# A mixture-of-experts layer in fp32: two experts' token columns gathered at once, and the down products by column halves

## The chip, the cores and the metric

The kernel runs on one core of one Trainium2 chip. The metric is the device time of one execution in microseconds (us). One core is used, so there is no exchange with others.

## The reference

One layer of a decoder on 256 tokens of width 1024: a mixer (a gated convolution beside chunked gated linear attention), then a mixture of 32 experts of which each token uses 4, then a final RMS norm. The part that matters here is the experts:

```
logits = xf @ w_router + b_router            # 256 x 32
top_v, top_i = lax.top_k(logits, 4);  gates = softmax(top_v)
for each expert e, for the tokens that chose it:
    gu   = x_e @ w_gate_up[e] + b_gate_up[e]         # 1024 -> 2048
    gate = min(gu[:, :1024], 7);  up = clip(gu[:, 1024:], -7, 7)
    glu  = gate * sigmoid(gate * 1.702)
    y[tokens] += gate_weight * (((up + 1) * glu) @ w_down[e] + b_down[e])
out = rmsnorm(x + y)
```

All numbers are float32. An expert has 1024 x 2048 weights for gate and up and 1024 x 1024 for down, 12.58 MB together, and the 32 experts have 402.7 MB. Everything is read once.

## The kernel before, in words

The mixer and the router run first, about 123 us. Then one pass over the experts, each as an item of at most 64 tokens (SLOTS; what more tokens an expert has goes to extra items after the last expert, of which this input needs none). An expert's weights are 6 chunks of 2.1 MB: chunks 0 to 3 hold gate and up, 4 and 5 hold down. A ring of 12 slots holds two experts' chunks. SyncE (SP) issues the loads in order on one queue; each waits until TensorE has counted the chunk that lay in its slot as used (`s_used`). Experts 6 to 13 and 22 to 27 are loaded in pairs of chunks (4 MB, line 572; at both edges of these ranges some more pairs, line 599), experts 14 to 21 in fours (8 MB, line 560); the first experts and the last two are loaded in chunks and smaller pieces. TensorE waits on the semaphore of a slot before the first product of its chunk.

What TensorE does for expert `it` is written out by hand in `products` and is the same for all experts:

- `gate_up`: 4 chunks, each 4 blocks of 128 rows, for each of which the 64 token columns `x_t` are the stationary operand and 512 weight columns the moving one, twice (two halves of the array side by side). Between the chunks it turns the gate matrix of this expert (`turn_gates`, result `p_t`) and, when ScalarE has copied a bank, the products (`turn`).
- `down`: 2 chunks, products into bank 0, 512 columns wide; VectorE and ScalarE make the activations meanwhile.
- `gather_next`: the rows of the next expert's tokens are picked out of `xs` by a 0/1 matrix `p_row` that VectorE made (scaled by the norm's factor), into bank 3. ScalarE copies them to `x_row`, TensorE turns them (`turn_gathered`, 4 transposes), and VectorE multiplies them by the norm's weights into `x_t`.
- `scatter`: ScalarE has copied bank 0 to `z`; the products of `p_t` and `z` are added to four banks y that hold the output of all 256 tokens.

The code for experts 0 and 1 is written out, that for 2 to 29 is a hardware loop over pairs (`InLoop`), and experts 30 and 31 are interleaved by hand in `products_last_two`, whose down weights come in pieces so that little is left after the last load. Three things are done once on the way: the down biases (`start_sums`) and the residual rows (`add_rows`) are added to the y banks in experts 4 and 5, and the final norm's weights are spread over the partitions (`broadcast_g`) in experts 12 and 13. In the program every fp32 product is two MATMUL instructions; a transpose is one.

## Time and profile before

| | before |
|---|---|
| median of 3 runs | 1015.89 us (1015.86 to 1016.98) |
| profiled execution, its own time | 1016.16 us |
| its span, first to last instruction | 1014.4 us |
| TensorE (PE) busy | 996.1 us, 98% |
| VectorE (DVE), ScalarE (ACT) busy | 284.5 us, 152.8 us |
| memory moved | 423.86 MB, mean 418 GB/s |
| chain that ended last, by engine | PE 87%, DMA 11% |

Busy times are sums over the instructions of an engine. The profiled execution lies 0.27 us over the median. TensorE works through a queue in order, and the end of a matmul is modelled, so that two engines (TensorE and the 16 DMA engines) can both look full; which of them the other waits for has to be read from single waits.

### The profile page before, as it was taken

To read this page: it belongs to the slowest core of one execution; us is meant where nothing else is said; L and a number is where in the kernel's file an instruction comes from. 1 tells how busy PE (TensorE), PEld (TensorE's weight loads), DVE (VectorE), ACT (ScalarE), POOL (GpSimd) and SP (SyncE) were. 2 spreads that over 40 slices of the span, in tenths; PEclk is the share of its full clock that TensorE was granted. 3 is DMA by queue.
4 is the path that set the end of the run, shared out by engine and by line. 5 is a ranking of instruction groups with operands and counts; after the bars stand their busy time and mean duration, and the time that the engine had idled before them with its cause. 6 is when DMAs were issued, how large, how long until landed. Compare 5 with 4: busy or idle time off the path is not lost.

```text
span 1014.4 us, 12715 instructions
## 1 busy us (share of the span) xinstructions
PE 996.1 (98%) x4940; PEld 414.9 (41%) x4940; DVE 284.5 (28%) x692; ACT 152.8 (15%) x324; POOL 14.8 (1%) x31
## 2 busy tenths in 40 slices
PE   9999999999999999999999999999999999999997
PEld 8889734333333333333333333332333333333334
DVE  4997522222221222222221122211222222122122
ACT  2421311111111111111111111111111111111112
POOL 3010000000000000000000000000000000000000
PEclk9999999999999999999999999999999999999999
DMA  9986999999999999999999999999999999999997
GB/s 368 426 371 263 390 402 425 427 433 425 430 432 432 433 425 434 430 433 442 437 432 432 437 429 439 429 439 421 424 434 430 433 433 432 433 421 431 426 419 283
DMA packets 23510, 423.86 MB, mean 418 GB/s; under 512 B 2872, under 2 KB 3520, under 8 KB 8000
## 3 DMA queue, kind: packets, MB, share of 16 engines
q1 hardware_dynamic: 22464, 422.09, 97.7%
q10 hardware_dynamic: 1024, 1.47, 0.4%
q8 instruction: 14, 0.23, 0.1%
q14 instruction: 8, 0.07, 0.0%
HBM read 422.51 MB, written 1.05 MB: 418 GB/s over the span
## 4 chain that ended last, share of the span: by engine, by line
PE 87%; DMA 11%; SPq 1%; issue 1%; DVE 0%; ACT 0%; POOLq 0%; POOL 0%; ACTq 0%; DVEq 0%; PEldq 0%
PE bank L2000 38%; PE bank L2027 20%; PE y L2071 5%; PE bank L1860 5%; DMA ring<-in_w_expert 5%; DMA ring<-in_w_fours 4%; PE bank L1628 4%; PE bank L2045 3%; DMA ring<-in_w_down_last 3%; PE y L1803 2%; PE bank L1935 2%; PE bank L1704 1%; PE bank L1621 1%; PE bank L2051 1%; PE y L1614 1%; PE bank L1803 1%
## 5 line engine op out<-in xcount | busy, mean ns | idle before, releaser
L2000 PE MATMUL bank<-ring,x_t 128*64 128x512 f32 x1984 | 447.3, 597 | 0.3 <-DVE x_t L1442 0.3
L2000 PEld LDWEIGHTS bank<-ring,x_t 128*64 128x64 f32 x1984 | 134.1, 137 | 262.6 <-issue 260.4
L2027 PE MATMUL bank<-ring,act 128*64 128x512 f32 (+1 forms) x968 | 224.6, 596 | 4.4 <-DMA ring<-in_w_fours 2.3
L1482 DVE TENSOR_TENSOR gu_b<-bank,bias_t 128x512 f32<-128x512 f32 x64 | 44.3, 692 | 322.4 <-PE bank L2045 322.4
L2027 PEld LDWEIGHTS bank<-ring,act 128*64 128x64 f32 x968 | 67.5, 137 | 129.8 <-issue 129.6
L931 ACT COPY gu_sb<-bank 128x512 f32<-128x512 f32 x64 | 37.4, 585 | 222.9 <-PE bank L2000 222.9
L1435 DVE TENSOR_TENSOR x_t<-bank,cols 128x512 f32<-128x512 f32 x30 | 20.7, 691 | 165.1 <-PE bank L1935 165.1
L2071 PE MATMUL y<-z,p_t 64*128 64x512 f32 (+1 forms) x248 | 59.7, 601 | 0.0
L1860 PE MATMUL bank<-x_sb,p_row 128*64 128x512 f32 x248 | 58.5, 592 | 0.0
L1421 DVE TENSOR_SCALAR p_row<-slot,rank,rstd 128x64 f32<-128x64 f32 x62 | 16.6, 311 | 147.7 <-PE bank L2051 147.7
L935 ACT ACTIVATE act<-gu_b 128x256 f32<-128x256 f32 x62 | 25.8, 416 | 190.4 <-DVE gu_b L1488 190.4
L2045 PEld LDWEIGHTS bank<-ident,gu_sb 128*128 128x128 f32 x256 | 26.8, 140 | 51.7 <-issue 51.3
L2045 PE MATMUL bank<-ident,gu_sb 128*128 128x128 f32 x256 | 42.0, 286 | 0.1
L927 ACT COPY p_t<-bank 128x256 f32<-128x256 f32 x31 | 11.5, 373 | 185.7 <-PE bank L2051 185.7
L1860 PEld LDWEIGHTS bank<-x_sb,p_row 128*64 128x64 f32 x248 | 17.8, 137 | 35.4 <-issue 35.4
L939 ACT COPY z<-bank 128x512 f32<-128x512 f32 x30 | 17.6, 586 | 85.5 <-PE bank L2027 85.5
L2071 PEld LDWEIGHTS y<-z,p_t 64*128 64x128 f32 x248 | 21.6, 186 | 18.8 <-issue 13.7
L1498 DVE TENSOR_TENSOR act<-act,gu_b 128x256 f32<-128x256 f32 x62 | 26.4, 425 | 6.5
L1493 DVE SCALAR_TENSOR_TENSOR gu_b<-gu_b 128x256 f32<-128x256 f32 x64 | 27.2, 425 | 2.2
L923 ACT COPY x_row<-bank 128x512 f32<-128x512 f32 x31 | 18.1, 585 | 63.0 <-PE bank L1860 63.0
L1935 PEld LDWEIGHTS bank<-ident,x_row 128*128 128x128 f32 x124 | 13.0, 141 | 31.2 <-issue 31.2
L1935 PE MATMUL bank<-ident,x_row 128*128 128x128 f32 x124 | 19.5, 280 | 4.8 <-PE bank L2027 4.6
(311 smaller groups left out, 549.1 us busy)
## 6 DMA issues: line engine op xcount, KB each, us to landing
ring<-in_w_expert SPq DMA_DIRECT2D x48, 4096.0 KB, 24.4
ring<-in_w_expert SPq DMA_DIRECT2D x33, 2048.0 KB, 14.6
ring<-in_w_expert SPq DMA_DIRECT2D x16, 1024.0 KB, 9.3
ring<-in_w_in SPq DMA_DIRECT2D x4, 2048.0 KB, 25.3
ring<-in_w_down_last SPq DMA_DIRECT2D x10, 512.0 KB, 19.6
ring<-in_w_out SPq DMA_DIRECT2D x2, 2048.0 KB, 27.4
ring<-in_w_expert SPq DMA_DIRECT2D x8, 512.0 KB, 6.4
ring<-in_w_down_last SPq DMA_DIRECT2D x3, 1024.0 KB, 35.7
```

Source lines behind the costliest of these rows:

```text
L931: act_e.copy(gu_sb[:, h, :], bank[h][:, :]).then_inc(s_guk, 1)
L1482: dve.tensor_tensor(gu_b[:, :, :, :], bank[2][:, :].rearrange("p (f a s) -> p a f s", a=2, f=4), bias_t[:, :, 4 * h:4 * h + 4, ds(e, 1)] . ...
L1493: dve.scalar_tensor_tensor(out=gu_b[:, 1, :, :], in0=gu_b[:, 1, :, :], scalar=1.0, in1=gu_b[:, 0, :, :], op0=ALU.add, op1=ALU.mult).then_i ...
L1498: dve.tensor_tensor(act_of(it)[:, 4 * h:4 * h + 4, :], act_of(it)[:, 4 * h:4 * h + 4, :], gu_b[:, 1, :, :], ALU.mult).then_inc(s_av, 1)
L1628: ins = mm(acc.rearrange("p a n -> p (a n)"), h[:, k, :], w[:, k, :], start=first and k == 0, stop=last and k == 3, skip_group_check=True)
L1803: ins = mm(acc, y[:, k, :], w[:, k, :], start=first and k == 0, stop=last and k == CT - 1, skip_group_check=True)
L1860: ins = mm(bank[3][a * SLOTS:(a + 1) * SLOTS, :], p_row[:, t, :], xs[:, t, a * HALF:(a + 1) * HALF], start=t == 0, stop=t == TT - 1)
L1935: ins = nc.tensor.transpose(bank[3][:, f * P:(f + 1) * P], x_row[:, f * P:(f + 1) * P], ident[:, :])
L2000: ins = mm(bank[h][a * SLOTS:(a + 1) * SLOTS, :], x_t_of(it)[:, k, :], w[:, kk, a, :], start=k == 0, stop=k == KT - 1)
L2027: ins = mm(bank[0][a * SLOTS:(a + 1) * SLOTS, c], act_of(it)[:, k, :], w[:, kk, a, c], start=k == 0, stop=k == KT - 1)
L2045: ins = nc.tensor.transpose(bank[2][:, f * P:(f + 1) * P], gu_sb[:, h, f * P:(f + 1) * P], ident[:, :])
L2071: ins = mm(y_ps[t][nn][:, c], p_t_of(it)[r, t * P:(t + 1) * P], z[r, c], start=first, stop=False, skip_group_check=True)
```

## The change

Four things.

- For experts 2 to 31 the token columns of two experts are gathered at once (`gather_pair`, in experts 1, 3, 5, ... 29): now `xs` is the stationary operand (128 x 128) and the two experts' 0/1 matrices side by side, `p_rows`, are the moving one (128 columns), so that the columns come out turned. The copy to `x_row`, the 4 transposes and the wait between them are gone. VectorE makes `x_pair` out of bank 3 in two halves (`keep_pair`), the second product waits for the first half.
- The down products are made by column halves: all rows of the chunk for columns 0 to 255 into bank 0, then for columns 256 to 511 into bank 1; ScalarE copies `z` in two halves, and `scatter` adds it in two halves.
- The spread of the final norm's weights (`broadcast_g`) moves from experts 12 and 13 to expert 30, the down biases (`start_sums`) from expert 4 to expert 1.
- In the first scatter only the first half resets a y bank. `bdn` lies elsewhere and is loaded after the gate biases and once the gates are there, not before them.

The core of the diff:

```diff
@@ build
-        gu_sb, x_t, p_row, p_gate = row((("gu_sb", [P, 2, HALF], f32), ("x_t", [P, KT, SLOTS], f32),
-                                         ("p_row", [P, TT, SLOTS], f32), ("p_gate", [P, TT, P], f32)), 8192, 16384)
+        gu_sb, x_pair = row((("gu_sb", [P, 2, HALF], f32), ("x_pair", [P, KT, 2, SLOTS], f32)), 8192, 16384)
+        x_t = at("x_t", [P, KT, SLOTS], 12288)
+        bdn = at("bdn", [P, HALF], 14336)
@@ load_biases (SP)
-                sp.wait_ge(s_lg, 2)
-                sp.dma_start(bdn[:, :], b_down).then_inc(s_bdn, 16)
                 sp.wait_ge(s_p0, 3)
                 sp.dma_start(bias_t[:, :, :, :], b_gate_up.rearrange("p (a f e) -> p a f e", a=2, f=F // P)).then_inc(s_bias, 16)
+                sp.wait_ge(s_gtk, 1)
+                sp.dma_start(bdn[:, :], b_down).then_inc(s_bdn, 16)
@@ ScalarE
-            def keep_z(it):
-                act_e.wait_ge(s_dn, it + 1)
-                act_e.copy(z[:, :], bank[0][:, :]).then_inc(s_z, 1)
+            def keep_z(it, extra):
+                for h in range(2):
+                    c = slice(h * QUARTER, (h + 1) * QUARTER)
+                    act_e.wait_ge(s_dn, down_done(it, h, extra))
+                    act_e.copy(z[:, c], bank[h][:, 0:QUARTER]).then_inc(s_z, 1)
@@ VectorE
+            def keep_pair(it):
+                for h in range(2):
+                    dve.wait_ge(s_xg, it + (2 + h))
+                    dve.tensor_tensor(x_pair[:, 4 * h:4 * h + 4, :, :].rearrange("p k o s -> p k (o s)"),
+                                      bank[3][:, :].rearrange("p (k s) -> p k s", k=4),
...
+                                      .broadcast_to([P, 4, P]), ALU.mult).then_inc(s_xt, 1)
@@ TensorE, down
-                    for a in range(2):
-                        for c in column_parts(it) if k in (5, 6) else (slice(0, HALF),):
-                            ins = mm(bank[0][a * SLOTS:(a + 1) * SLOTS, c], act_of(it)[:, k, :], w[:, kk, a, c],
-                                     start=k == 0, stop=k == KT - 1)
+                    for a in range(2):
+                        ins = mm(bank[h][a * SLOTS:(a + 1) * SLOTS, 0:QUARTER], act_of(it)[:, k, :], w[:, kk, a, c],
+                                 start=k == 0, stop=k == KT - 1)
@@ TensorE
+            def gather_pair(it, h):
+                if h == 0:
+                    pe.wait_ge(s_p, number(it) + 2)
+                    pe.wait_ge(s_ptk, number(it) + 1)
+                else:
+                    pe.wait_ge(s_xt, number(it) + 2)
+                for k in range(4 * h, 4 * h + 4):
+                    for t in range(TT):
+                        ins = mm(bank[3][:, k % 4 * P:(k % 4 + 1) * P], xs[:, t, k * P:(k + 1) * P],
+                                 p_rows[:, t, :, :].rearrange("p o s -> p (o s)"), start=t == 0, stop=t == TT - 1)
+                ins.then_inc(s_xg, 1)
@@ products
+                if known == 1:
+                    start_sums()
+                if isinstance(it, InLoop) and it.odd == 0:
+                    pe.wait_ge(s_xt, number(it) + 2)
...
-                down(it, 4, range(0, 2))
+                down(it, 4, 0, range(0, 2), extra)
                 turn(it, 1)
-                down(it, 4, range(2, 4))
-                if following is not None:
+                down(it, 4, 0, range(2, 4), extra)
+                down(it, 4, 1, range(4), extra)
+                next_pair = known == 1 or isinstance(it, InLoop) and it.odd == 1
+                if known == 0:
                     gather_next(it)
+                if next_pair:
+                    gather_pair(it, 0)
                 pe.wait_ge(s_av, number(it) * 2 + 2)
-                down(it, 5, range(4))
-                if following is not None:
-                    turn_gathered(following)
-                scatter(it)
+                for h in range(2):
+                    down(it, 5, h, range(4), extra)
+                if known == 0:
+                    turn_gathered(1)
+                if next_pair:
+                    gather_pair(it, 1)
+                scatter(it, extra)
```

How TensorE's instructions stand in the hardware loop, in the second expert of a pair, from the second half of chunk 2 on (a row here is a product of two instructions, or one transpose, by the source line; ring_51 is where the down chunks lie). Before:

```order
L2000 MATMUL bank<-ring_51,x_t 64x512 x12
L2027 MATMUL bank<-ring_51,act 64x512 x4
L2040 REGISTER_ALU
L2045 MATMUL bank<-ident,gu_sb 128x128 x4
L2027 MATMUL bank<-ring_51,act 64x512 x4
L2056 REGISTER_ALU
L1860 MATMUL bank<-x_sb,p_row 64x512 x4
L2027 MATMUL bank<-ring_51,act 64x512 x8
L1935 MATMUL bank<-ident,x_row 128x128 x4
L2071 MATMUL y<-z,p_t 128x512 x4
```

After:

```order
L2028 MATMUL bank<-ring_51,x_pair 64x512 x12
L2047 MATMUL bank<-ring_51,act 64x256 x4
L2062 REGISTER_ALU
L2067 MATMUL bank<-ident,gu_sb 128x128 x4
L2047 MATMUL bank<-ring_51,act 64x256 x12
L2102 REGISTER_ALU
L2108 MATMUL bank<-p_rows,x_sb 128x128 x8
L2047 MATMUL bank<-ring_51,act 64x256 x16
L2108 MATMUL bank<-p_rows,x_sb 128x128 x8
L2094 MATMUL y<-z,p_t 128x256 x8
```

The gather of 4 wide products and the 4 transposes became 16 products of 128 columns in two groups; in the first expert of a pair both are gone. Down has 32 products of 256 columns where it had 16 of 512, the scatter 8 where it had 4.

TensorE's instructions in expert 1, from its start to its first turned products, before:

```order
L2000 MATMUL bank<-ring_50,x_t 64x512 x8
L2051 MATMUL bank<-ident,p_gate 128x128 x2
L2000 MATMUL bank<-ring_50,x_t 64x512 x8
L2000 MATMUL bank<-ring_51,x_t 64x512 x4
L2045 MATMUL bank<-ident,gu_sb 128x128 x4
```

And after:

```order
L2028 MATMUL bank<-ring_50,x_t 64x512 x8
L2005 MATMUL y<-bdn,gates_t 128x512 x4
L2073 MATMUL bank<-ident,p_gate 128x128 x2
L2028 MATMUL bank<-ring_50,x_t 64x512 x8
L2028 MATMUL bank<-ring_51,x_t 64x512 x4
```

The 4 products of the down biases now stand after the expert's first chunk; they stood in expert 4.

SyncE's queue around the two bias loads, with what each waits for (first_p_row_ready is `s_p0`, gates_t_ready is `s_gtk`). Before:

```order
L579 DMA early_quarter<-in_w_expert 128x1024 [waits partial_logits_ready]
L552 DMA ring_51<-in_w_expert 128x1024 [waits block_product_ready]
L583 DMA bdn<-in_b_down 128x512 [waits logits_ready]
L585 DMA bias_t<-in_b_gate_up 128x512 [waits first_p_row_ready]
L552 DMA ring_49<-in_w_expert 128x1024 [waits first_chunks_quarter_used] x3
```

After:

```order
L593 DMA early_quarter<-in_w_expert 128x1024 [waits partial_logits_ready]
L566 DMA ring_51<-in_w_expert 128x1024 [waits block_product_ready]
L597 DMA bias_t<-in_b_gate_up 128x512 [waits first_p_row_ready]
L599 DMA bdn<-in_b_down 128x512 [waits gates_t_ready]
L566 DMA ring_49<-in_w_expert 128x1024 [waits first_chunks_quarter_used] x3
```

The load of `bdn` moved behind that of `bias_t` and has another wait; the first refill of a ring slot stands right behind it. From there on SyncE's queue is the same, load by load.

## Rows read from the trace of the kernel before

**Rows 1.** The page: the engines' busy time, and TensorE's group that waits most.

```profile
PE 996.1 (98%) x4940; PEld 414.9 (41%) x4940; DVE 284.5 (28%) x692; ACT 152.8 (15%) x324; POOL 14.8 (1%) x31
...
L2027 PE MATMUL bank<-ring,act 128*64 128x512 f32 (+1 forms) x968 | 224.6, 596 | 4.4 <-DMA ring<-in_w_fours 2.3
```

**Rows 2.** Waits of SyncE's queue: total us, times, longest.

```profile
SPq L572 <- PE bank L2000: 233.9, 28, 9.9
```

**Rows 3.** DMA view of 150 to 210 us: rate, and loads with median us to landing.

```profile
DMA packets 2069, 25.58 MB, mean 426 GB/s; under 512 B 234, under 2 KB 234, under 8 KB 234
...
ring<-in_w_expert SPq DMA_DIRECT2D x11, 2048.0 KB, 12.4
```

**Rows 4.** The same view of 730 to 850 us.

```profile
DMA packets 1780, 51.81 MB, mean 432 GB/s; under 512 B 199, under 2 KB 199, under 8 KB 199
...
ring<-in_w_expert SPq DMA_DIRECT2D x14, 4096.0 KB, 42.8
```

**Rows 5.** Chain from 290 to 350 us: start us, us, what.

```profile
292.39 3.58 PE bank L2000 x16
...
311.70 1.72 PE bank L1860 x8
313.42 3.46 PE bank L2027 x16
...
317.01 0.63 PE bank L1935 x4
317.64 1.92 PE y L2071 x8
319.55 3.59 PE bank L2000 x16
```

**Rows 6.** Chain in the mixer, 128 x 128 products of 128 columns (two instructions each).

```profile
76.29 5.36 PE bank L1621 x48
```

**Rows 7.** Chain in expert 1, whose down and scatter are partly in halves.

```profile
171.57 3.51 PE bank L2027 x24
...
175.85 2.03 PE y L2071 x16
```

**Rows 8.** Chain: down biases in expert 4, one half of the final weights' spread.

```profile
240.01 1.07 PE y L1977 x8
...
462.93 1.08 PE bank L2115 x8
```

**Rows 9.** Windows: stretch, its us, busy times, clock share, DMA share, GB/s last.

```profile
122.00:126.00 4.00, 3.71 (x22) 1.49 (x21) 1.73 (x7) 1.59 (x2) 0.00 (x0) 1.00 0.78 243
134.00:138.00 4.00, 4.00 (x22) 1.37 (x20) 1.37 (x5) 0.42 (x1) 0.00 (x0) 1.00 1.04 432
```

**Rows 10.** Timeline around 122 us: the gates, and the first refills.

```profile
122.08 0.22 DVE L1414 TENSOR_TENSOR gates<-ex,ngt 128x64 f32<-128x64 f32 x1
...
124.21 24.09 SPq L552 DMA_DIRECT2D ring<-in_w_expert  x15
```

**Rows 11.** DMA view: the 2 MB load issued within 157 to 159 us.

```profile
ring<-in_w_expert SPq DMA_DIRECT2D x1, 2048.0 KB, 9.7
```

**Rows 12.** The same view of 90 to 91 us.

```profile
DMA packets 0, 0.00 MB, mean 0 GB/s; under 512 B 0, under 2 KB 0, under 8 KB 0
ring<-in_w_expert SPq DMA_DIRECT2D x1, 2048.0 KB, 7.3
```

**Rows 13.** TensorE's timeline: two waits for loads; in brackets the idle time before.

```profile
692.60 3.53 PE L2027 MATMUL bank<-ring,act 128*64 128x512 f32 x8 [2.27 <-DMA ring<-in_w_fours]
...
886.96 1.94 PE L2027 MATMUL bank<-ring,act 128*64 128x512 f32 x8 [1.78 <-DMA ring<-in_w_expert]
```

**Rows 14.** The chain at the end.

```profile
967.78 27.57 DMA ring<-in_w_down_last
...
1006.71 0.92 PE y L2151 x12
```

**Rows 15.** Window 1005 to 1006 us, columns as in rows 9.

```profile
1005.00:1006.00 1.00, 1.00 (x23) 1.00 (x21) 0.54 (x2) 0.65 (x3) 0.00 (x0) 1.00 0.00 0
```

163 lines of the change are left out of this document (87 added, 76 removed).

## The prediction

> **What bounds the kernel now.** I read the page first. TensorE is busy 98% of the span and its costliest waiting group is idle only 4.4 us in all [rows 1]; SyncE's queue waits hundreds of microseconds on TensorE's counts [rows 2]. That looks like a kernel bound by TensorE. But a queue that waits before it issues the next load may still have loads in flight, so I asked the DMA view of two stretches. Between 150 and 210 us the engines move 426 GB/s, and a 2 MB load lands 12.4 us after its issue [rows 3]. Between 730 and 850 us they move 432 GB/s, and a load lands 42.8 us after its issue [rows 4]. The time to landing more than tripled while the rate stayed. So the loads queue up behind each other, the more the later; the rate is that of the DMA engines themselves, and no earlier issue raises it. SyncE's waits on TensorE are waits at the tail of a queue that never runs dry.
>
> The balance confirms it. One expert's weights are 12.58 MB, at 432 GB/s 29.1 us, 58.2 us a pair. TensorE needs 319.55 - 292.39 = 27.16 us for an expert, 54.3 us a pair [rows 5]. It is faster than its loads by 3.9 us a pair and lives on the ring of two experts that was full when it began. The ring runs dry late: the first wait for a load is at 692.60 us (2.27 us idle), another at 886.96 us (1.78 us) [rows 13], and the last links of the chain before TensorE's final work are a load issued at 967.78 us that landed 27.57 us later, at 995.34 us [rows 14]. Behind it come TensorE's last pieces, until 1007.63 us, and the final norm. In 1005 to 1006 us nothing is loaded any more [rows 15]. From 134 us, when the rate is 432 GB/s [rows 9], to about 1004 us the load stream is full. **The time is: when the stream fills up, plus bytes by rate, plus the tail.** TensorE's work per expert is not in this sum as long as it stays under 29.1 us and loses no start.
>
> **The change part by part, TensorE's work.** Per pair of experts, two gathers of 1.72 us go, and two groups of 4 transposes of 0.63 us with the gap of 0.13 us before each (from 313.42 + 3.46 to 317.01) [rows 5]: 4.96 us removed. Added are 16 products, 32 instructions, of 128 columns with a full 128 x 128 stationary operand. The mixer has that form: 48 in 5.36 us, 0.112 us each [rows 6]; 3.57 us. The bound below is the array's rate in the down products, 3.46 us for 16 instructions of 512 columns of which two run side by side [rows 5], so 0.108 us for 128 columns on the whole array: 3.46 us. The bound above is a transpose's price, 0.63 us for 4 or 0.158 us each [rows 5]: 5.04 us. I take the mixer's row, which has the same shape and pairs of instructions.
>
> The halves of down and scatter have a sample in the kernel before, expert 1. There 8 more instructions in the second down chunk make 3.51 us out of 3.46, and a scatter in halves takes 2.03 us against 1.92 [rows 5, 7]. For 32 more instructions per expert that is 0.20 us, with the scatter 0.31 us per expert, 0.62 us a pair.
>
> Sum: -4.96 + 3.57 + 0.62 = -0.77 us a pair (bounds -0.88 and +0.70), from 54.3 to 53.5 us, and -11.6 us over the 15 pairs (bounds -13 and +10.5). At both bounds a pair stays under the 58.2 us of its loads. So this term is hidden behind the load stream, worth 0 in the time. It moves TensorE's waits instead: the ring runs dry earlier, by my estimate near 600 us in place of 690, and TensorE then idles about 5 us a pair.
>
> A page makes the gather cheaper. The Trainium skill, "TensorE: Matmul & The Clock Gate", section "Back-to-back issue gap", gives about 81 ns for a sustained matmul of 128 columns. By it the gather of a pair would cost 2.6 us and the pair would gain 1.7 us, 26 us in all; the row has 112 ns for our fp32 form, and by either the work is hidden.
>
> **The start of the stream** is where TensorE does count. At 122 to 126 us DMA is busy 78% of the time [rows 9], since the refills of the ring begin only when TensorE has used its first quarter chunks, the first at 124.21 us [rows 10]. The load of `bdn` now waits for the gates, done at 122.08 + 0.22 = 122.30 us [rows 10]. SyncE then issues one load and has 1.9 us before the refill's wait opens. Cost 0. If the gates came 2 us later, the stream would start later by the rest.
>
> After that the queue is shortest near 158 us: a 2 MB load issued there lands after 9.7 us [rows 11], while one issued into an idle queue takes 7.3 us [rows 12]. So TensorE may be 2.4 us late there before the stream breaks. What does the change add by then? Half a chunk of down in expert 0 is released about 1 us later (half of the second column half must be done as well), but not the whole chunk. In expert 1 the down biases come after the first chunk, 1.07 us [rows 8]. At its end 3.57 us of gather replace 1.72 + 0.76, +1.09 us, and halves add 0.6 us over the two experts. That makes 1.1 to 1.4 us at 158 us and 2.2 to 2.8 us at the start of expert 2, where the queue is longer (12.4 us in the median, margin 5 us [rows 3]). No break; cost 0, bound above 1 us if each wait behind these adds some tenths. Expert 2 has no gather at all and wins it back.
>
> Other waits. The turned columns' first half must be copied by VectorE, one instruction, before the second gather; between lie 16 down products, 3.5 us [rows 5]. Behind that wait stand the scatter and the next expert. ScalarE's first half of `z` is copied while the second half is multiplied, the second under the first half's scatter (half of 2.03 us [rows 7]). All covered; with the cover gone each would cost under 1 us a pair, which the 4.7 us of slack take.
>
> **The tail.** `broadcast_g` now stands in expert 30, two times 1.08 us [rows 8], in place of a gather and its transposes, 2.48 us [rows 5]: -0.3 us, and before the point at 995.34 us where TensorE waits for a load anyway [rows 14]. Behind that point nothing changed but names. Cost 0.
>
> **The sum.** The profiled execution: 1016.16 us = 1014.4 us of span + 1.76 us around it. Plus 0 at the start, 0 in the stream, 0 in the tail: 1016.2 us. It lay 0.27 us over the median of the runs, so as a median 1015.9 us.
>
> **The rivals.**
>
> 1. *The loads are held back by the ring after all*, and TensorE's work counts: 1016.2 - 11.6 = 1004.6 us (bounds 1003 and 1026). For it: the 98%, and SyncE's waits [rows 1, 2]. Against it: the rate did not change when the queue got three times as long [rows 3, 4]. Chance 0.04. A smaller gain, because some stretch of the stream is not full, 0.02.
>
> 2. *The clock falls at the end* (the slower side). When TensorE had waited 2.27 us, the next 8 instructions took 3.53 us in place of 1.94 us: they ran at 1.2 GHz, not 2.4 [rows 13]. After 1.78 us it stayed. TensorE will now idle from about 600 us on, at every load. In the middle that costs nothing: a pair has 4.7 us of slack, and a fall costs 1.6 us. But the last 11 us after 995.34 us have no slack, and in the last chunks TensorE will have idled more than before. One fall there gives 1017.8 us, still within 0.2%; two give 1019.4 us, slower. It decides if the granted clock is at half within the last 20 us. Against it: from 985 us on both kernels have the same loads to wait for and the same work. One fall 0.05, two or more 0.04. The Trainium skill, "TensorE: Matmul & The Clock Gate", section "HAM oscillation — how this bites in real kernels", tells of a matmul kernel that waits for a DMA between bursts and falls to the low clock at every burst; by that rule it would be common here from 600 us on. The one fall in the trace agrees with the mechanism.
>
> 3. *The early stream breaks*, because expert 1 got longer by more than I count: the price is the delay beyond 2.4 us at 158 us, or beyond about 4 us at the start of expert 2, one for one. Some tenths to 1 us (within 0.2%): 0.06. Over 2 us, at 1018 us or more: 0.05.
>
> 4. *No change*, my forecast: 1015.9 us, own range 1015.0 to 1017.0. Chance 0.74.
>
> **How the numbers follow.** A measurement of this kernel can tell about 0.2%, 2.0 us, from no change. Faster by more: 0.06 (rival 1). Slower by more: 0.09 (two falls, a late start). Within: 0.85. The range for 8 in 10 takes in one fall, a small break and half a microsecond below the lowest run: 1014.6 to 1018.2 us.
>
> **What would show it.** Right: DMA at 430 to 432 GB/s from 134 us on with the last load landing within 1 us of before; a pair of experts at 53 to 54 us in TensorE's chain before the first wait; the first wait near 600 us; TensorE's waits on loads rising from about 5 us to 15 to 25 us, its busy time down by about 10 us; the chain that ended last with more DMA in it. Wrong: windows between 130 and 200 us with less than 420 GB/s (rival 3); a granted clock under 1.00 after 985 us (rival 2); a span shorter by the 11 us that TensorE saved (rival 1), which would mean that the rate of the DMA engines is not what I take it for.

## The result, and the profile after

The changed kernel takes 1020.28 us (median; 1019.71 to 1021.33), the kernel before, run beside it, 1015.88 us (1015.45 to 1017.58). The ratio is 1.0038, 95% interval 1.0028 to 1.0048: slower by 4.4 us. The forecast was 1015.9 us, with a range up to 1018.2.

| | after |
|---|---|
| profiled execution, its own time | 1020.32 us (4.16 more) |
| its span | 1018.6 us (4.2 more) |
| TensorE (PE) busy | 993.6 us, 98% |
| VectorE, ScalarE busy | 284.5 us, 140.0 us |
| memory moved | mean 416 GB/s |
| chain that ended last, by engine | PE 78%, DMA 21% |

The page of the changed kernel, engines and the two weight groups of TensorE (its down products have the line 2047 now):

```profile
PE 993.6 (98%) x6244; PEld 532.6 (52%) x6244; DVE 284.5 (28%) x692; ACT 140.0 (14%) x324; POOL 14.8 (1%) x31
...
L2028 PE MATMUL bank<-ring,x_pair 128*64 128x512 f32 x1920 | 433.4, 597 | 3.3 <-DMA ring<-in_w_expert 1.8
...
L2047 PE MATMUL bank<-ring,act 128*64 128x256 f32 x1920 | 226.7, 387 | 6.9 <-DMA ring<-in_w_fours 3.9
```

TensorE's work shrank, as meant: 2.5 us less busy, 3.3 + 6.9 us idle at loads where [rows 1] have 4.4 in the one group. It issues 6244 instructions where [rows 1] have 4940. This number, which the prediction does not mention, comes back below. The forecast was a busy time lower by about 10 us.

The pair of experts in the chain, 450 to 505 us (start us, us, what), against [rows 5]:

```profile
450.79 0.14 issue
450.93 2.02 PE bank L2108 x16
452.95 1.93 PE y L2094 x16
454.88 3.58 PE bank L2028 x16
...
471.46 6.22 PE bank L2047 x56
477.68 0.14 issue
477.82 2.00 PE y L2094 x16
...
499.15 1.98 PE bank L2108 x16
501.13 3.63 PE bank L2047 x32
504.76 0.14 issue
```

From 450.79 to 504.76 us a pair takes 53.97 us. The forecast was 53.5, before it was 54.3. So TensorE saves 0.36 us a pair, 5.4 us over 15 pairs, and none of it reaches the time. Its busy time falls by less than that, since its clock falls three times in this kernel before 1000 us, and once in the kernel before; each fall makes it busy for some 1.6 us more.

Where do the 4.2 us come from? Three points split the span: the first refill of the ring (the load at 124.21 us before [rows 10], at 123.77 us after), the landing of the last load, and the last store. The first and second come from the trace's single loads.

| us | before | after | more |
|---|---|---|---|
| first refill issued at | 124.21 | 123.77 | -0.44 |
| from there to the last load's landing ("the stream") | 881.33 | 882.92 | +1.59 |
| from there to the end of TensorE's last y product ("the lag") | 2.27 | 3.46 | +1.19 |
| from there to the issue of the last store | 3.55 | 3.55 | 0 |
| from there to the end of the span | 3.06 | 4.88 | +1.82 |
| sum | 1014.4 | 1018.6 | +4.2 |

The first refill varies between 123.2 and 124.7 us in the runs below, whatever the kernel, so the -0.44 is chance.

The last two rows can be read in the timeline of SyncE at the end (start us, us of the issue). First of the kernel before:

```profile
1011.35 0.40 SPq L684 DMA_DIRECT2D out<-y_out  x1
```

and of the changed one:

```profile
1013.70 0.40 SPq L698 DMA_DIRECT2D out<-y_out  x1
```

1014.4 - 1011.35 = 3.1 us and 1018.6 - 1013.70 = 4.9 us. The two kernels store the same 4 pieces of 256 KB. The DMA view of 1008.5 to 1016 us shows what is beside them. Before:

```profile
q1 hardware_dynamic: 576, 1.05, 37.7%
...
out<-y_out SPq DMA_DIRECT2D x4, 256.0 KB, 2.4
```

After:

```profile
q1 hardware_dynamic: 558, 1.02, 36.8%
q8 instruction: 2, 0.03, 1.9%
q14 instruction: 1, 0.01, 0.4%
...
out<-y_out SPq DMA_DIRECT2D x4, 256.0 KB, 2.9
```

Two packets of 16 KB of TensorE's instructions ("q8 instruction") are fetched by DMA engines in this window, one at 1010.4 us, ahead of the stores, and one at 1015.1 us, among them. By the experiments below they are the code of the extra items, which this input never runs, and of what follows. The trace's single packets show what comes late. In the kernel before the stores' last packet ends at 1013.66 us, 2.3 us after the last issue. In the changed kernel almost all of them have ended by 1016.0 us, 2.3 us after its last issue as well; but from 1016.05 to 1017.72 us packets of 2 KB follow one another singly, most of them 84 ns long. They look like what one of the 16 DMA engines had left over; the trace does not name the engine, so this is not shown.

The lag is seen in TensorE's timeline (idle time before in brackets). Its last wait in the changed kernel:

```profile
887.93 1.08 PE L2047 MATMUL bank<-ring,act 128*64 128x256 f32 x8 [1.99 <-DMA ring<-in_w_expert]
...
889.70 4.28 PE L2047 MATMUL bank<-ring,act 128*64 128x256 f32 x24
```

and in the kernel before, after the wait at 886.96 us [rows 13], three more places:

```profile
981.61 5.66 PE L2000 MATMUL bank<-ring,x_t_last 128*64 128x512 f32 x24
987.92 1.95 PE L2127 MATMUL bank<-ring,act 128*64 128x256 f32 x16 [0.66 <-DMA ring<-in_w_down_last]
...
994.19 3.14 PE L2127 MATMUL bank<-ring,act 128*64 128x256 f32 x24
```

The timeline gives idle time in brackets only from 0.15 us on. The first and the last row hide a shorter stop each: elsewhere these groups take 5.37 and 2.81 us, and inside the first row lies the landing of a load at 985.29 us, inside the last the landing at 995.34 us of [rows 14]. That makes 0.29 + 0.66 + 0.33 = 1.3 us, all the slack that TensorE had between 888 us and the last landing. In the changed kernel it never waits for a load again; it is late by then. The windows 889 to 893 us (columns as in [rows 9]) show one reason. Before:

```profile
889.00:893.00 4.00, 4.00 (x22) 1.55 (x23) 2.04 (x5) 0.42 (x1) 0.00 (x0) 1.00 0.99 426
```

After:

```profile
889.00:893.00 4.00, 4.00 (x23) 2.26 (x24) 2.03 (x5) 0.42 (x1) 0.00 (x0) 0.57 1.05 451
```

The granted clock is 0.57 in the mean of these 4 us, so TensorE ran mostly at 1.2 GHz, and 24 instructions that take 2.81 us elsewhere took the 4.28 us of the row above, 1.5 us more (1.6 with the four transposes ahead of them). The other reason is the spread of the final weights, the first two rows of this chain, which is TensorE's own from 887.93 us on:

```profile
969.35 1.08 PE bank L2157 x8
...
974.01 1.08 PE bank L2157 x8
...
1006.29 2.77 PE bank L2182 x48
1009.06 0.92 PE y L2193 x12
```

Where [rows 14] have a DMA that lands at 995.34 us, no load stands in the chain any more.

The stream, last, is thinner early. Windows 134 to 220 us, before and then after:

```profile
134.00:220.00 86.00, 85.53 (x416) 31.13 (x414) 18.81 (x50) 11.07 (x22) 0.00 (x0) 1.00 1.01 427
```

```profile
134.00:220.00 86.00, 85.52 (x534) 40.41 (x532) 18.85 (x50) 10.31 (x23) 0.00 (x0) 1.00 1.01 419
```

8 GB/s less over 86 us is 86 x 8 / 430 = 1.6 us of load time. Note that the DMA share is 1.01 in both: the share does not show this loss, the rate does. Most of it falls right behind the point at 158 us that the prediction had picked. In the windows of 4 us from 158 to 170 us the rate was 442, 424 and 430 GB/s before and is 371, 393 and 373 now, about 1.5 us of load time. The first of the three, before and after:

```profile
158.00:162.00 4.00, 4.00 (x22) 1.39 (x20) 1.51 (x4) 1.00 (x2) 0.00 (x0) 1.00 1.06 442
```

```profile
158.00:162.00 4.00, 4.00 (x22) 1.42 (x20) 0.86 (x2) 0.58 (x1) 0.00 (x0) 1.00 1.01 371
```

### The profile page after: what moved, and what is told of

Its sections match the earlier page's. It is cut to its first block, busy times and chain, and to the rows that moved or that the text cites. A ratio compares the mean times of both kernels' runs of the same rounds, so it can differ in the third digit from the quotient of the medians.

```text
span 1018.6 us, 15150 instructions
## 1 busy us (share of the span) xinstructions
PE 993.6 (98%) x6244; PEld 532.6 (52%) x6244; DVE 284.5 (28%) x692; ACT 140.0 (14%) x324; POOL 14.8 (1%) x31
## 4 chain that ended last, share of the span: by engine, by line
PE 78%; DMA 21%; issue 0%; DVE 0%; ACT 0%; POOLq 0%; POOL 0%; ACTq 0%; SPq 0%; PEldq 0%; DVEq 0%
PE bank L2028 33%; PE bank L2047 18%; DMA ring<-in_w_fours 12%; DMA ring<-in_w_expert 9%; PE bank L2108 5%; PE y L2094 4%; PE bank L1656 4%; PE bank L2067 3%; PE y L1831 2%; PE bank L1732 1%; PE bank L1649 1%; PE bank L2169 1%; PE y L1642 1%; PE bank L2073 1%; PE bank L1831 1%
## 5 line engine op out<-in xcount | busy, mean ns | idle before, releaser
L2028 PE MATMUL bank<-ring,x_pair 128*64 128x512 f32 x1920 | 433.4, 597 | 3.3 <-DMA ring<-in_w_expert 1.8
L2028 PEld LDWEIGHTS bank<-ring,x_pair 128*64 128x64 f32 x1920 | 129.3, 136 | 247.0 <-issue 240.0
L2047 PE MATMUL bank<-ring,act 128*64 128x256 f32 x1920 | 226.7, 387 | 6.9 <-DMA ring<-in_w_fours 3.9
L2047 PEld LDWEIGHTS bank<-ring,act 128*64 128x64 f32 x1920 | 135.0, 139 | 94.2 <-issue 37.1
L2108 PE MATMUL bank<-p_rows,x_sb 128*128 128x128 f32 x480 | 61.1, 280 | 2.4 <-PE bank L2047 2.4
L2108 PEld LDWEIGHTS bank<-p_rows,x_sb 128*128 128x128 f32 x480 | 55.8, 191 | 14.6 <-issue 14.6
L2094 PE MATMUL y<-z,p_t 64*128 64x256 f32 x480 | 59.9, 388 | 2.2 <-PE bank L2047 2.2
L2094 PEld LDWEIGHTS y<-z,p_t 64*128 64x128 f32 x480 | 46.2, 186 | 12.3 <-issue 8.4
L955 ACT COPY z<-bank 128x256 f32<-128x256 f32 x60 | 22.3, 372 | 162.4 <-PE bank L2047 162.4
L2028 PE MATMUL bank<-ring,x_t 128*64 128x512 f32 x128 | 28.8, 597 | 0.3 <-DVE x_t L1465 0.3
```

The source lines that it names most:

```text
L2028: ins = mm(bank[h][a * SLOTS:(a + 1) * SLOTS, :], x_columns(it, k), w[:, kk, a, :], start=k == 0, stop=k == KT - 1)
L2047: ins = mm(bank[h][a * SLOTS:(a + 1) * SLOTS, 0:QUARTER], act_of(it)[:, k, :], w[:, kk, a, c], start=k == 0, stop=k == KT - 1)
L2094: ins = mm(y_ps[t][nn][:, c], p_t_of(it)[r, t * P:(t + 1) * P], z[r, c], start=first and h == 0, stop=False, skip_group_check=True)
L2108: ins = mm(bank[3][:, k % 4 * P:(k % 4 + 1) * P], xs[:, t, k * P:(k + 1) * P], p_rows[:, t, :, :].rearrange("p o s -> p (o s)"), start=t = ...
```

## The experiments

Each was timed beside the kernel before on the same chip. Ratios are to the kernel before; its median there was between 1016.25 and 1016.63 us. "Stream", "lag" and "store" (issue of the last store to the end of the span) are measured in each trace as in the table above. They are those of one execution, the time is a median. For "after, no start_sums" the profiled execution was the slowest of its eleven, 1020.59 us, for "both of these" the fastest, 1016.71 us; there the three columns do not explain the median.

| run | time, us | ratio, 95% interval | stream | lag | store |
|---|---|---|---|---|---|
| before | 1015.88 | 1 | 881.33 | 2.27 | 3.1 |
| after | 1020.28 | 1.0038, 1.0028 to 1.0048 | 882.92 | 3.46 | 4.9 |
| after, once more | 1020.35 | 1.0035, 1.0021 to 1.0048 | 883.02 | 3.34 | 5.0 |
| after, no spread | 1019.63 | 1.0032, 1.0020 to 1.0044 | 883.06 | 2.26 | 4.8 |
| after, no code for extra items | 1017.75 | 1.0016, 1.0007 to 1.0025 | 883.06 | 3.09 | 3.1 |
| both of these | 1017.62 | 1.0012, 1.0003 to 1.0021 | 882.57 | 2.35 | 3.1 |
| after, down undivided | 1020.49 | 1.0038, 1.0024 to 1.0051 | 885.92 | 2.32 | 3.1 |
| after, experts 0 and 1 undivided | 1017.96 | 1.0015, 1.0006 to 1.0024 | 882.43 | 2.51 | 3.1 |
| before, spread late | 1016.96 | 1.0003, 0.9994 to 1.0012 | 881.63 | 2.60 | 3.1 |
| before, longer code behind the last expert | 1018.47 | 1.0016, 1.0007 to 1.0025 | 882.07 | 2.27 | 4.6 |
| before, longer code in the loop | 1016.49 | 1.0000, 0.9991 to 1.0009 | 881.84 | 2.26 | 3.1 |
| before, 1.8 us of delay in expert 1 | 1018.00 | 1.0016, 1.0007 to 1.0026 | 883.63 | 2.27 | 3.1 |
| before, 3.5 us | 1020.39 | 1.0037, 1.0023 to 1.0051 | 885.23 | 2.29 | 3.1 |
| before, 10.6 us | 1026.63 | 1.0100, 1.0085 to 1.0116 | 892.13 | 2.28 | 3.1 |
| before, 20.9 us | 1039.47 | 1.0226, 1.0212 to 1.0240 | 902.37 | 2.29 | 5.0 |
| before, start_sums moved | 1016.60 | 1.0001, 0.9992 to 1.0010 | 882.94 | 2.23 | 3.1 |
| after, no start_sums | 1018.54 | 1.0022, 1.0013 to 1.0031 | 883.03 | 2.96 | 5.0 |
| after, start_sums later | 1020.62 | 1.0040, 1.0026 to 1.0054 | 882.90 | 3.99 | 5.1 |
| the same, experts 0 and 1 undivided | 1018.83 | 1.0023, 1.0014 to 1.0032 | 883.74 | 2.27 | 3.1 |

### The tail: the spread of the weights

After without the spread (both calls of `broadcast_g` left out, `g_bc` filled with ones, so the final norm's weights are not applied):

```
-                broadcast_g(0)
...
-                broadcast_g(1)
...
-                    dve.tensor_copy(g_bc[:, h * HALF:(h + 1) * HALF], bank[3][:, :]).then_inc(s_gbk, 1)
+                    dve.memset(g_bc[:, h * HALF:(h + 1) * HALF], 1.0).then_inc(s_gbk, 1)
```

> The changed kernel without the two spreads of the final norm's weights in expert 30 (the work is left out: the weights are taken as ones). Theory 1, no slack at the end: after its last wait for a load at 887.9 us the changed kernel's TensorE never waits again, so its 2 x 1.08 us of spread count there, until it meets the load stream, which ends 1.15 us later than before: 1018.2 to 1019.1 us, and the last y product at most 1.2 us after before's 1007.6 us. Theory 2, the load stream and the stores alone make the time: 1020.3 us, no change.

The lag is back at 2.26 us, although the clock falls after the same wait (its windows of 889 to 893 us). In time it gave less than expected: 1019.63 us, a ratio of 1.0032 where the changed kernel has 1.0038 or 1.0035, and the intervals overlap. So the lag is seen in the profile, and its worth in the median stays unproved.

```profile
889.00:893.00 4.00, 4.00 (x22) 2.33 (x22) 2.04 (x5) 0.42 (x1) 0.00 (x0) 0.57 1.01 434
```

The other way round, the kernel before with the spread moved to expert 30 (two groups of gate and up are split to make room, and the transposes of the gather stand a little earlier):

```
-                    with pe.If(it.first == SPREAD_AT):
-                        ...
-                        broadcast_g(it.odd)
...
 # products_last_two
+                broadcast_g(0)
+                gate_up(b, 0, range(2))
+                pe.wait_ge(s_gbk, 1)
+                broadcast_g(1)
                 turn(a, 1)
...
+                gate_up(b, 0, range(2, 4))
+                pe.wait_ge(s_gbk, 2)
```

> The kernel before with the two spreads moved from experts 12 and 13 to expert 30, nothing else. Theory 1: before had 0.66 us of TensorE slack at the end (its wait at 987.3 us), so of 2.16 us moved there 1.5 us count: 1017.4 us. Theory 2: 1015.9 us.

It costs 0.33 us of lag and nothing measurable in time (ratio 1.0003), where 1.5 us were expected: the expectation took the 0.66 us in brackets for all the slack. With the 1.3 us counted above, 0.9 of the 2.16 us are left over; TensorE's end came 1.0 us later, and the last load 0.6 us later. So neither the late spread nor the fall of the clock makes the lag alone. With the fall and no spread it is 2.26 and 2.35 us. With the spread and no fall it is 2.60 us here, and 2.27 to 2.51 us in the three variants of the changed kernel whose clock is 1.00 from 889 to 893 us (row below: the run with experts 0 and 1 undivided). With both it is 3.0 to 4.0 us in five kernels.

```profile
889.00:893.00 4.00, 4.00 (x36) 2.43 (x33) 2.04 (x5) 0.42 (x1) 0.00 (x0) 1.00 0.99 426
```

### The stores: the length of the code

After without TensorE's code for extra items (this input has none; with such items the output would lack them):

```
-            with pe.If(n > E):
-                with pe.Fori(E, n) as it:
-                    ...
```

> The changed kernel without TensorE's code for extra items, which this input never enters. In the changed kernel the last store took 4.5 us to land and not 2.7, and a TensorE instruction fetch of 16 KB lay on the DMA engines at 1015.1 us, during the stores; before had none there. Theory 3, that fetch delays the store: 1.8 us less, 1018.5 us. If the store's delay has another cause: 1020.3 us.

Both together, no spread and no such code:

> The changed kernel without the spreads (left out, weights taken as ones) and without TensorE's code for extra items. If the three parts add (stream 1.6 us, TensorE's lag at the end 1.2 us, store 1.8 us), only the stream's is left: 1.5 us over before, 1.0015. If there is a fourth part, more.

And the reverse, the kernel before with 32 products more in that code, which never runs:

```
             with pe.If(n > E):
                 with pe.Fori(E, n) as it:
+                    for _ in range(32):
+                        mm(bank[3][:, 0:P], ones[:, :], ones[:, :], start=True, stop=True)
```

> The kernel before with 32 more products (128 TensorE instructions) in the code for extra items, which is never entered. Theory 3: if the end of the code now lies over a fetch border, a fetch appears during the stores, the last store lands 1.8 us later and the time is 1.8 us more, with nothing else changed; if no fetch appears there, the time is that of before. Against theory 3: a fetch during the stores and no later landing, or a late landing without a fetch.

The DMA view of 1008.5 to 1016 us of the run without the code:

```profile
q1 hardware_dynamic: 576, 1.05, 37.8%
q14 instruction: 1, 0.01, 0.3%
...
out<-y_out SPq DMA_DIRECT2D x4, 256.0 KB, 2.4
```

and of the padded kernel before:

```profile
q1 hardware_dynamic: 574, 1.05, 38.2%
q8 instruction: 2, 0.03, 1.6%
q14 instruction: 1, 0.01, 0.3%
...
out<-y_out SPq DMA_DIRECT2D x4, 256.0 KB, 2.9
```

Taken out, the span ends 3.1 us after the last store's issue instead of 4.9, and the ratio falls from 1.0038 to 1.0016, 2.2 us. Put in, where no instruction runs that did not run before, it ends 4.6 us after, and the kernel before loses 1.8 us (1018.47 against 1016.63). One fetch by itself does no harm: in the run with experts 0 and 1 undivided one is at 1010.6 us, ahead of the stores, and the span ends 3.1 us after the last issue. It is the fetch that starts among the stores: seven of the profiles in the table have one there, with 4.6 to 5.1 us, the other twelve have none, with 3.0 to 3.1 us. That the place of this fetch sets the end is shown from both sides. Why a packet that took 0.9 to 1.5 us costs 1.5 to 2.0 us is not.

### The halves of the down products

After, with down, `z` and scatter undivided:

```
-                c = slice(h * QUARTER, (h + 1) * QUARTER)
-                        ins = mm(bank[h][a * SLOTS:(a + 1) * SLOTS, 0:QUARTER], act_of(it)[:, k, :], w[:, kk, a, c],
+                        ins = mm(bank[0][a * SLOTS:(a + 1) * SLOTS, :], act_of(it)[:, k, :], w[:, kk, a, :],
```

> The changed kernel with down and scatter undivided again (512 columns in one bank), the pair gather and the late spread kept. Theory 1: from the last wait on, three experts' halves cost 0.3 us each, and fewer TensorE instructions are fetched: 1019.3 us. If the halves are the whole loss (a rival): 1016 us. Theory 2 with the stream delayed by the fetch of more instructions: about 1 us less, 1019.3 us as well, but then the last load lands 1 us earlier and TensorE's end does not.

The pair gather then makes TensorE slower than before, 55.3 us a pair. Waits in the expert that has no gather, in TensorE's timeline of that run:

```profile
481.26 3.65 PE L2046 MATMUL bank<-ring,act 128*64 128x512 f32 x16 [0.63 <-DVE act L1519]
485.65 1.99 PE L2091 MATMUL y<-z,p_t 64*128 64x512 f32 x8 [0.73 <-ACT z L953]
```

The gather of the next expert had filled the time in which VectorE makes the activation and ScalarE copies `z`. In an expert without a gather both stand open, 1.4 us a pair, and the halves cover them again. They are part of the pair gather, not an edit beside it. This kernel has no late fetch and a short lag, and is as slow as the changed one, 1020.49 us where 1016 or 1019.3 was expected: its stream is 3.0 us longer still.

### The early stream

The loads' landings, counted from each kernel's first refill and against the same load of the kernel before, drift between 150 and 285 us in the changed kernel, and then stay within 0.02 us up to the load that lands at 916 us (worked out from single loads; us later than before):

```
landing before, us    147.2  157.9  172.7  182.7  212.1  246.1  324.0  673.1  916.1
after                 -0.17  -1.08  -0.11   1.05   1.43   1.45   1.41   1.42   1.42
longer code in loop   -1.32  -0.50  -0.50   0.03   0.65   0.68   0.64   0.65   0.65
start_sums moved      -0.32  -0.50   0.72   0.40   0.44   0.56   0.53   0.53   0.54
1.8 us of delay        0.11  -0.38   0.51   0.99   0.99   1.00   1.26   1.26   1.27
3.5 us of delay       -0.48  -1.00   1.58   2.88   2.88   3.19   3.46   3.46   3.46
```

The first column shows how far a figure of one profile can be trusted: at 147 us the kernels already lie up to 1.4 us apart, and the kernel with longer code in the loop runs nothing there that the kernel before does not run. In a second profile of the changed kernel the landings also make a step of 0.5 us at 343 us.

Theory A was the code again (five fetches of 16 KB between 142 and 223 us instead of four, each on one of 16 engines), theory B TensorE's delay in experts 1 and 2. The first try was the changed kernel with down undivided in experts 0 and 1 only:

```
+                if isinstance(it, int) and it < PE_FROM:
+                    ...  # as before: 512 columns into bank[0], one z, one scatter
```

> The changed kernel with down and scatter undivided in experts 0 and 1 alone, so 144 TensorE instructions fewer before the loop. Theory A, the fetches of TensorE's longer code hold up the load stream: one fetch of 16 KB less between 140 and 220 us, the last load 881.3 to 881.7 us after the first refill as in before (changed kernel 882.9), and the code's end lies elsewhere, so that the last store may land in 2.7 us: 1.5 to 3.3 us less than the changed kernel. Theory B, the stream is late because TensorE is late in experts 1 and 2: still 882.9 us, and nothing gained but the store's part if any.

Beside it stood the changed kernel unaltered:

> The changed kernel once more, as the measure for the other kernels of this call: slower than before by a factor of 1.0038, the last store landing 4.5 us after its issue, the last y product of TensorE 3.3 us after the last load. If the slow store was an accident of one execution, it lands after 2.7 us here.

The stream went from 883.02 to 882.43 us only; most of the 2.4 us gained came from the end, where shorter code moved the fetches ahead of the stores and the clock did not fall. This did not tell the theories apart. So each was put into the kernel before by itself, code first: 32 products in each half of the loop body, never run.

```
+                    with pe.If(it.first == 1000):
+                        for _ in range(32):
+                            mm(bank[3][:, 0:P], ones[:, :], ones[:, :], start=True, stop=True)
```

> What is tested: why the change's load stream, from the first refill's issue to the last load's landing, takes 882.9 us where the kernel before takes 881.3. The kernel before, with 32 more products in each half of the loop body over pairs of experts, behind a condition that is never true: they are fetched but not run, so TensorE is late nowhere. Theory A (each 16 KB fetch of TensorE's instructions occupies one of the 16 DMA engines for about 1 us, and the change's longer code needs five before 230 us where the kernel before needs four): one fetch more before 230 us, stream 881.8 to 882.9, time 1016.5 to 1018 where the kernel before has 1016.6. Theory B (TensorE is some 2.5 us late in experts 1 and 2, slots of the ring come free later and fewer loads stand in the queue between 155 and 200 us): stream 881.2 to 881.7, time within 0.5 us of the kernel before.

Then the delay:

```
+                if known == 1:
+                    for _ in range(12):
+                        mm(bank[1][:, :], ident[:, :], xs[:, 0, 0:HALF], start=True, stop=True)
```

> The kernel before, with 12 products of 512 columns more in expert 1 (ident by xs into bank 1, each about 0.22 us from its rows, 2.6 us in sum; the sums over experts are not touched). So TensorE is as late at 155 to 190 us as in the change, with the code of the kernel before. Theory B: the load that goes out at 158 us has 8 to 8.5 us from issue to landing instead of 9.7, and the stream takes 882.3 to 883, time 1017.5 to 1018.3. Theory A: the latency falls too, but the stream stays at 881.2 to 881.7 and the time within 0.5 us of the kernel before, since TensorE has hundreds of us to catch up.

> The same with 24 such products, 5.2 us in sum. Theory B: the queue runs nearly dry at 158 and at 182 us, and the stream takes some 2 to 4 us more than before (883.3 to 885.5), time 1018.5 to 1021. Theory A: stream 881.2 to 882 still, since loads of up to 9 us from issue to landing stand in the queue at 158 us and 5.2 us do not empty it.

The dose was mistaken. I had divided the rows of the expert products, of which two run side by side on 64 columns of the array each; these use all 128 columns. TensorE's timeline of the run with 12:

```profile
154.06 10.57 PE L2086 MATMUL bank<-x_sb,ident 128*128 128x512 f32 x24
```

10.57 us, 0.88 us each, and the stream became 10.8 us longer; 24 of them gave 20.9 and 21.0 us. So with large delays every us arrives. Smaller doses:

> The kernel before with 2 more products of 512 columns and 128 weight columns in expert 1; by the run with 12 of them each takes 0.88 us, so 1.8 us. Theory B2 (TensorE's delay in expert 1 passes to the load stream one to one, since the queue has no time to spare there): stream 883.0 to 883.5 where the kernel before has 881.3, time about 1.8 us more. Theory B (the queue has some 2.5 us to spare at 158 us, the 9.7 us from issue to landing less the 7.2 us of a load that finds the queue empty): stream 881.3 to 881.8, time within 0.5 us of the kernel before.

> The same with 4 such products, 3.5 us. Theory B2: stream 884.8 to 885.4, time 3.5 us more. Theory B: stream 882.3 to 883.0, time some 1 to 1.5 us more, and the first refill of expert 1 lands 7.2 to 7.5 us after its issue.

Windows 134 to 220 us of 1.8, of 3.5 and of 10.6 us of delay:

```profile
134.00:220.00 86.00, 85.53 (x414) 31.30 (x412) 18.32 (x48) 10.91 (x22) 0.00 (x0) 1.00 1.00 417
```

```profile
134.00:220.00 86.00, 85.53 (x408) 31.47 (x406) 18.34 (x48) 10.71 (x22) 0.00 (x0) 1.00 0.99 409
```

```profile
134.00:220.00 86.00, 85.53 (x392) 32.21 (x390) 16.34 (x44) 10.06 (x20) 0.00 (x0) 1.00 0.90 375
```

427, 417, 409, 375 GB/s are 2.0, 3.6 and 10.4 us of load time lost, for 1.8, 3.5 and 10.6 us of delay. The times follow: +1.75, +4.1, +10.3 us. Theory B's slack of 2.5 us in the queue is not there. The load behind the delay shows why; the DMA view of 157 to 161 us with 1.8 us of delay:

```profile
DMA packets 174, 1.34 MB, mean 336 GB/s; under 512 B 23, under 2 KB 23, under 8 KB 23
...
ring<-in_w_expert SPq DMA_DIRECT2D x1, 2048.0 KB, 7.5
```

7.5 us is close to the 7.3 of an idle queue [rows 12], and the rate falls to 336 GB/s, in the changed kernel (8.3 us) to 371, where the kernel before has 432 with the 9.7 us of [rows 11]. The rate sags while loads are still in flight.

The edits of the change that make such a delay were then taken one by one. Start_sums out of the changed kernel (the experts' down bias is left out):

```
                 if known == 1:
-                    start_sums()
+                    pe.wait_ge(s_gtk, 3)
+                    pe.wait_ge(s_bdn, 16)
```

> The changed kernel without its four start_sums products in expert 1 (the experts' down bias is left out of the output), so TensorE is 1.07 us earlier at the first refill of expert 1. Theory B2 (delay in expert 1 passes one to one): stream 881.8 to 882.0 where the change has 882.9 to 883.1, time 1 us less than the change's (1.0025 of the kernel before instead of 1.0035). Theory B: less than 0.3 us of it, since at 158 us the queue still has slack and the later delay of the pair gather (at 184 us) stays; stream 882.6 to 883.

Start_sums alone moved to expert 1, in the kernel before:

```
+                if known == 1:
+                    start_sums()
                 turn_gates(it)
...
-                        if it.odd == 0:
-                            start_sums()
```

> The kernel before with only the move of start_sums from expert 4 to the start of expert 1 (1.07 us of TensorE ahead of expert 1's first refill). If this move is what costs the stream: landings 0.8 to 1.3 us later than in the kernel before from 170 us on, stream 882.1 to 882.6, time 0.7 to 1.3 us more. If the queue covers 1 us there: stream 881.3 to 881.6, no change in time.

Start_sums of the changed kernel at the end of expert 1, ahead of the pair gather, and the same with down of experts 0 and 1 undivided:

```
-                if known == 1:
-                    start_sums()
...
+                if known == 1:
+                    start_sums()
                 if next_pair:
                     gather_pair(it, 0)
```

> The changed kernel with start_sums at the end of expert 1, ahead of the pair gather (at about 171 instead of 154 us). If the move ahead of expert 1's first refill is what costs: landings at 212 to 246 us where they are in the kernel before within 0.3 us, where the change has them 1.45 us later, and time 1 us less than the change's, 1.0022 to 1.0027 of the kernel before. If any delay in experts 1 and 2 costs the same: as the change, 1.0035.

> sums_later with down products and scatter of experts 0 and 1 undivided. The last store is not delayed by an instruction fetch (2.65 us instead of 4.5) as in the run with undivided halves alone, and the stream is within 0.6 us of the kernel before; what stays is the pair's lag at the end. Time 1.0005 to 1.0012 of the kernel before; by the rival (any delay costs the same) 1.0015 as without the sums moved.

The move alone costs nothing in time (ratio 1.0001). In its profile the landings come 0.5 us later from 180 us on, 0.8 us behind 980 us, and only the very last one 1.6, which makes the 882.94 us. Left out of the changed kernel, the windows 134 to 220 us are back at 426 GB/s, and the ratio goes from 1.0035 to 1.0022 (the intervals overlap). The profiled execution, the slowest of its eleven, has a stream as long as with them: it lost 0.9 us elsewhere, between 246 and 345 us. Moved to the end of expert 1, the loss came there in full, 2.0 us by 212 us, and the time did not fall. So the place of this edit is not the cause. That it is the sum of TensorE's delays in experts 0 to 2 fits these runs and those with a delay of 1.8 and 3.5 us; how much start_sums has of it was not shown. None of the versions beats the kernel before; the nearest that keeps the pair gather and leaves nothing out is the one with experts 0 and 1 undivided, 1.0015.

## Why the prediction was wrong, point by point

**What bounds the kernel: right.** The time is the load stream between a start and a tail. TensorE's saving of 5.4 us left no trace in it; the waits for loads grew from 2.3 + 2.2 + 0.7 = 5.2 to 3.9 + 3.0 + 1.8 + 1.4 = 10.1 us. From 285 to 916 us both kernels land every load at the same distance, within 0.02 us of a constant, in the two profiles compared. The rival that the ring holds the loads back is excluded for that stretch.

**The pair's price: right in kind, off in size.** -0.36 us a pair, within the bounds of -0.88 and +0.70, where -0.77 was taken. 16 instructions of the gather took 1.98 to 2.02 us, about 0.125 us each, where the mixer's row of 0.112 [rows 6] was used; 4.00 in place of 3.57 us for the 32 is the whole difference. That no size here mattered is because the term is hidden. By the Trainium skill, "TensorE: Matmul & The Clock Gate", section "Back-to-back issue gap", they would have been cheaper than either, 81 ns; the trace does not agree for this fp32 form. First wait near 600 us: 595.3 us. Waits of 15 to 25 us: 10.1.

**The tail, "Behind that point nothing changed but names. Cost 0": wrong.** The failed step is "before the point at 995.34 us where TensorE waits for a load anyway". I read the DMA link in the chain [rows 14] as slack without asking how much. It does wait there, for 0.3 us, and with the stops of 0.29 and 0.66 us ahead of it 1.3 us are all that lies behind 888 us. Against these stood the spread's 2.16 us and one fall of the clock of 1.6 us. The gathers and halves gave some 1.0 us back in this stretch, an estimate from rows: four gathers with their transposes, 4 x 2.48 us, became two pair gathers of 4.0 us and three experts with halves at 0.31 us. (The prediction set the spread against one whole gather, -0.3 us, but half of a pair gather stands in expert 29 for it.) That is 2.16 + 1.6 - 1.0 - 1.3 = 1.5 us by which TensorE is later against the loads; measured were 1.2 us. Without the spread, or without the fall, the remainder is below zero or near it, as the lags of 2.26 to 2.60 us show.

Rival 2 had the mechanism and the price, 1.6 us, but put the place at "the last 20 us": the fall was at 889 us, 117 us before the last landing, and still counts, since no wait lies behind it that could absorb it. Of the changed kernel's six waits for loads the three of 1.96 to 1.99 us were each followed by a fall, those of 0.99, 1.39 and 1.79 us by none. The length alone does not decide it: in the run with longer code in the loop TensorE waited 2.91 us and the clock stayed, and in the run with start_sums moved 2.80 us. So the fall behind 888 us could not be forecast from the length of the wait; it came in both profiles of the changed kernel. The rule of the Trainium skill named with rival 2, "TensorE: Matmul & The Clock Gate", section "HAM oscillation — how this bites in real kernels", says that a wait for a DMA between bursts brings the low clock; here it did at half of the waits.

**The stores: not in the prediction at all, +1.8 us.** The sum counted instructions by their duration on TensorE. 1304 more instructions in execution are also more code, and where the fetches of code fall moved with it. This is the largest term, shown in both directions. No sign or rival of the prediction could have pointed at it.

**The start of the stream: the mechanism of rival 3 was right, its threshold wrong.** "So TensorE may be 2.4 us late there before the stream breaks" is the failed step. The delays were forecast well (1.1 to 1.4 us at 158 us, measured 1.1 from the first refill; 2.2 to 2.8 at expert 2, measured 2.8). But 1.8 us of delay cost 1.75 us and 3.5 us cost 4.1. The excess of a load's latency over that of an idle queue was taken as time that could be lost; the rate begins to sag before it is used up. Of the forecast's signs, windows under 420 GB/s, this one showed, but it was set too loosely: the kernel before has 406 GB/s at 130 to 140 us and 418 at 150 to 160 us. What tells the two apart is 160 to 170 us, 368 GB/s against 433.

**What stays open.** How the stream's 1.6 us divide between delay and code. Code alone gave 0.5 us in a profile and none in time; a delay of 1.1 us alone gave 0.5 us in its landings and none in time. Between 0 and 1.8 us of delay the loss is not linear, and the stream of one profile varies by some 0.5 us (881.3 to 882.1 us, mean 881.7, in four kernels whose early TensorE work is that of before; 882.6 to 883.1 us, mean 882.9, in five that have the changed start). By these means the stream is 1.2 us longer, and not 1.6. Why `sums_later` lost as much as the change with an undisturbed 158 us is only argued: its load at 184 us landed 7.9 us after its issue, near the 7.3 us of an idle queue. Why the clock fell after some waits of about 2 us and not after others was not found: in the run with experts 0 and 1 undivided it fell after none of three, 1.96, 1.96 and 1.98 us.

The sum of the profiled executions closes: -0.4 (earlier first refill) + 1.6 (stream) + 1.2 (lag) + 1.8 (stores) = 4.2 us. That it does so to a tenth is in part luck, since the first two terms vary by about half a microsecond from profile to profile.

## What to carry to other kernels

- A link "DMA" in the chain at the end does not say how much slack the waiting engine had. Read the idle time in its timeline, in brackets and in groups that take longer than the same group elsewhere, from its last long wait to the end, and set every edit and every possible fall of the clock behind that wait against it.
- In this kernel, which lives on its load stream, the first loads after the start had the least margin: 1.8 us of delay there cost 1.75 us. Keep added work out of the compute engine until the queue is long, and judge that stretch by GB/s: its DMA share was 1.01 at 419 and at 427 GB/s.
- Code that never runs cost 1.8 us here, where its fetch fell among the last stores. After an edit that changes the number of instructions, look at the instruction queues' packets in the DMA view of the last 10 us.

## What the runs showed of the hardware that I had not expected

- A fetch of TensorE's instructions is a 16 KB packet on the DMA engines that carry the data. Where one started during the 4 stores of 256 KB, the span ended 4.6 to 5.1 us after the last store's issue, in all seven profiles that had one there, and 3.0 to 3.1 us after it in the twelve that had none.
- An fp32 product of 128 x 128 stationary values and 512 columns took 0.88 us (10.57 us for 12). The expert products, 64 stationary columns each and two side by side, take 3.58 / 8 = 0.45 us each.
- In the changed kernel waits of 1.96 to 1.99 us that ended at 635.5, 693.6 and 887.9 us were each followed within 1.5 us by a fall of the granted clock; the kernel before stayed at full clock after 1.78 us and fell after 2.27 us. But the length of the wait does not decide it. With longer code in the loop the clock stayed at 1.00 after this wait, and 8 instructions took 1.94 us, their time at 2.4 GHz:

```profile
693.24 1.94 PE L2027 MATMUL bank<-ring,act 128*64 128x512 f32 x8 [2.91 <-DMA ring<-in_w_fours]
```
